# A hybrid RWKV-7, GLA and MLA trunk: all projections of the normalized input in pairs by seven products

## The chip, the cores and the metric

The kernel runs on one core of a Trainium2 chip. The metric is the device time of one execution in microseconds (us). Data and arithmetic are float32.

## The reference, cut to what matters

Two layers run over 640 tokens: 512 of a grid and 128 of a prompt. In each layer the input is normalized and modulated, and one wide matrix w_in projects it to everything that the three branches need. The outputs of the branches are gated by a sigmoid of another part of the same projection, summed, and projected again.

```python
mod = (jax.nn.silu(cvec) @ w_mod + b_mod)[:, None, :]
shift, scale, gate = jnp.split(mod, 3, axis=-1)
h = rmsnorm(x, norm_g) * (1 + scale) + shift
proj = h @ w_in
(rw_r, rw_k, rw_v, rw_wd, rw_ad, rw_g, gl_q, gl_k, gl_v, gl_ad, gl_g,
 ml_qd, ml_kvd, ml_kpe, ml_g, merge) = jnp.split(proj, IN_SPLITS, axis=-1)
...
y_a = (o_a * jax.nn.silu(rw_g)) @ lp['rw_out']      # RWKV-7, forwards and backwards over the tokens
y_b = (o_b * jax.nn.silu(gl_g)) @ lp['gla_out']     # gated linear attention, both ways
y_c = (o_c * jax.nn.silu(ml_g)) @ lp['mla_out']     # attention over a compressed cache
g_a, g_b, g_c = jnp.split(jax.nn.sigmoid(merge), N_BRANCH, axis=-1)
return x + gate * ((g_a * y_a + g_b * y_b + g_c * y_c) @ lp['w_out'])
```

## The kernel before

The normalized input lies in SBUF as hT: 8 tiles of 128 features by 640 tokens. A **unit** is 128 output columns of a projection, 8 weight tiles of 128x128. Units stream from memory through a ring of five slots, unit n in slot n modulo 5; the SP engine asks for unit n when unit n − 5 has been used (L483). On TensorE `project()` makes one unit directly: eight matmuls with 512 columns and eight with 128. ACT copies the 128x640 result out of PSUM; for the gates (items g, gg, mg) ACT makes a sigmoid (L1263) and DVE multiplies it with the value in PSUM (L1552, `gates`).

The order is written out by hand in lists. FIRST_ITEMS are the four units at a layer's start. A layer then goes through four pairs of RWKV heads, **stage p** = 0 to 3. In it BESIDE[p] names four units that TensorE projects while DVE, ACT and a few small matmuls prepare the stage's factors: kkss is the norm sum of the keys, a cumulated decay follows as a scan (L1654), and for each direction d DVE makes the factors, among them the key factor from the activation w_a (L1557 and a product, L1552). When they are done (semaphore dve_fac) TensorE turns them (L585) and works through five token tiles in the steps (0, 1), (2, 3) and (4,). The last step has a long chain of small 64x64 matmuls with DVE and ACT in between; there `project_some` puts pieces of the two units of BESIDE_PROMPT[p] between them, and in layer 0 the modulation weights of the next layer pass through the ring in the same place. At the stage's end DVE finishes the output with a root from ACT and the gate.

Then come the unit kvd, the GLA branch, whose seven levels per quarter have pieces of nine units between them (GLA_FILL), the MLA branch with seven merge units (MLA_MERGE), two at its start and five at fixed steps of its loop, and the output stage. L1439 is ACT's exponential of a level, L1241 and L1245 are the two halves of a root on ACT.

Only the output stage works in pairs: `winograd` takes two units (256 output columns) as a 2x2 block matrix and makes their result by seven products, each of four matmuls with 320 columns, in place of eight block products. For this Pool makes four sums of the weights of a pair, 128x512 each (L523, L525, L526, L530, in `sums`), and once per layer four sums of the blocks of hT (L535 to L540); ACT copies three products and DVE adds the others up in 128x320 corners (`corners`, L1549). Twelve pairs per layer, mb, mc and wo, are made so. Helper lines are one for all: L582 is every matmul, L585 every transpose, L1549 an add, L1552 a product, L1556 and L1557 a scaling, L1560 a scale and add on DVE, L1250 a copy on ACT.

## Time and profile before

| | |
|---|---|
| time, median of 3 runs (lowest, highest) | 2675.94 us (2674.91, 2677.42) |
| the profiled execution, its time | 2676.53 us |
| its span | 2674.7 us |
| mean granted TensorE clock | 0.994 |
| TensorE matmuls busy | 2555.6 us (96%) |
| DVE busy | 1258.9 us (47%) |
| ACT busy | 889.7 us (33%) |
| Pool busy | 182.0 us (7%) |

A share of 96% over the span says which engine is the bound on the whole; it does not say how much idle time stands behind it in a single stage. That is read from the timeline of a stage, where one sees when another engine has its result ready and when TensorE takes it up.

### The profile page before, as it was taken

Reading aid. Unit: us, or ns where it says so; the run is one execution under the profiler, and the core shown is the slowest. Engines: PE = TensorE matmul, PEld = TensorE weight load, DVE = VectorE, ACT = ScalarE, POOL = GpSimd, SP = SyncE. Lnnn points to the kernel's source line nnn. Section 1 sums busy time; section 2 is a strip of 40 time slices with the busy share of each in tenths; the row PEclk is TensorE's granted clock in tenths of the full one; section 3 lists DMA queues with packets and bytes.
Section 4 is the critical chain, followed back from the end, with each engine's and each line's share of the span. In section 5 each row is a group of like instructions: output and inputs, shape, how many; then the busy total and the mean of one; then the engine's idle time right before and its main releaser. Section 6 shows DMA issues by size and latency. Waiting matters only on the chain.

```text
span 2674.7 us, 49682 instructions
## 1 busy us (share of the span) xinstructions
PE 2555.6 (96%) x21544; PEld 1732.9 (65%) x21544; DVE 1258.9 (47%) x2465; ACT 889.7 (33%) x1446; POOL 182.0 (7%) x164
## 2 busy tenths in 40 slices
PE   7999999999999999999999999999999999999997
PEld 3675857667666566666657767685866666566664
DVE  3545536364577444222336464554538735432233
ACT  3424323142454544111024242424334545421111
POOL 0000000000000002221300000000000000122122
PEclk9999999999999999999999999999999999999999
DMA  8102020111110000321321010101011010012212
GB/s 309 41 18 92 7 90 25 62 53 38 69 31 29 26 16 17 118 70 64 111 77 33 10 43 2 50 3 42 10 32 35 29 30 12 25 42 71 63 71 77
DMA packets 34983, 136.61 MB, mean 51 GB/s; under 512 B 4496, under 2 KB 4656, under 8 KB 34128
## 3 DMA queue, kind: packets, MB, share of 16 engines
q1 hardware_dynamic: 31392, 118.18, 13.0%
q0 software_dynamic: 3376, 15.24, 1.6%
q8 instruction: 174, 2.85, 0.4%
q14 instruction: 41, 0.34, 0.0%
HBM read 126.43 MB, written 6.98 MB: 50 GB/s over the span
## 4 chain that ended last, share of the span: by engine, by line
PE 84%; DVE 7%; ACT 5%; issue 2%; DMA 1%; POOL 0%; SPq 0%; ACTq 0%; DVEq 0%; POOLq 0%
PE psum L582 82%; PE psum L585 2%; DMA ring<-units 1%; DVE tmp L1549 1%; DVE m_nm L2046 1%; DVE tmp L1552 1%; ACT tmp L1250 1%; ACT tmp L1502 1%; DVE acts L1549 1%; DVE tmp L1560 1%; DVE tmp L1556 1%; ACT L1245 0%; DVE tmp L1939 0%; ACT L1241 0%; DVE acts L1552 0%
## 5 line engine op out<-in xcount | busy, mean ns | idle before, releaser
L582 PE MATMUL psum<-hT,ring 128*128 128x512 f32 (+2 forms) x3264 | 942.5, 441 | 16.8 <-DMA ring<-units 8.4
L582 PEld LDWEIGHTS psum<-hT,ring 128*128 128x128 f32 x3264 | 523.8, 191 | 418.5 <-issue 375.4
L582 PE MATMUL psum<-tmp 64*64 64x64 f32 (+9 forms) x10624 | 703.9, 259 | 42.6 <-DVE tmp L1552 11.4
L582 PEld LDWEIGHTS psum<-tmp 64*64 64x64 f32 (+3 forms) x10624 | 553.9, 149 | 159.0 <-issue 57.9
L1250 ACT ACTIVATE tmp<-psum 128x512 f32<-128x512 f32 (+7 forms) x490 | 252.7, 519 | 1006.7 <-PE psum L582 932.4
L1250 ACT ACTIVATE acts<-psum 128x640 f32<-128x640 f32 (+4 forms) x206 | 109.4, 531 | 320.0 <-PE psum L582 297.6
L582 PE MATMUL psum<-acts,ring 128*128 128x512 f32 (+1 forms) x768 | 210.8, 434 | 0.0
L1549 DVE TENSOR_TENSOR tmp<-psum,tmp 128x256 f32<-128x256 f32 (+2 forms) x184 | 75.7, 412 | 243.0 <-PE psum L582 208.3
L1549 DVE TENSOR_TENSOR tmp<-tmp,psum 128x320 f32<-128x320 f32 x120 | 56.4, 486 | 264.2 <-PE psum L582 202.1
L582 PEld LDWEIGHTS psum<-acts,ring 128*128 128x128 f32 x768 | 118.6, 191 | 94.7 <-issue 92.1
L1549 DVE TENSOR_TENSOR tmp<-tmp 128x320 f32<-128x320 f32 (+2 forms) x214 | 135.6, 660 | 5.0
L582 PE MATMUL psum<-tmp,ring 128*128 128x320 f32 x448 | 124.8, 432 | 0.0
L585 PE MATMUL psum<-con_sb,tmp 128*128 128x128 f32 x696 | 107.2, 279 | 14.3 <-DVE tmp L1556 13.9
L582 PE MATMUL psum<-acts 64*64 64x64 f32 (+3 forms) x2448 | 109.8, 228 | 5.9 <-DVE acts L1549 3.8
L2046 DVE TENSOR_REDUCE m_nm<-psum 128x1 f32<-128x768 f32 (+1 forms) x80 | 65.8, 822 | 100.7 <-PE psum L582 99.7
L582 PEld LDWEIGHTS psum<-tmp,ring 128*128 128x128 f32 x448 | 85.0, 190 | 35.1
L1716 DVE COPY_PREDICATED tmp<-masks_sb,psum 128x512 f32<-128x512 uint8 x160 | 105.4, 723 | 0.7
L582 PE MATMUL psum<-tmp,acts 128*128 128x320 f32 (+2 forms) x576 | 104.4, 350 | 0.6
L1552 DVE TENSOR_TENSOR tmp<-tmp,acts 128x320 f32<-128x320 f32 (+1 forms) x160 | 88.6, 586 | 34.5 <-ACT tmp L1439 29.1
L582 PEld LDWEIGHTS psum<-acts 64*64 64x64 f32 (+2 forms) x2448 | 93.9, 138 | 12.0 <-DVE acts L1549 9.7
L585 PEld LDWEIGHTS psum<-con_sb,tmp 128*128 128x128 f32 x696 | 78.4, 141 | 35.0 <-DVE tmp L1556 24.2
L1502 ACT ACTIVATE tmp<-psum,m_nm 128x768 f32<-128x768 f32 (+1 forms) x80 | 63.6, 795 | 90.7 <-DVE m_nm L2046 83.7
(164 smaller groups left out, 2157.7 us busy)
## 6 DMA issues: line engine op xcount, KB each, us to landing
ring<-units SPq DMA_DIRECT2D x210, 512.0 KB, 3.6
small_sb<-small SPq DMA_DIRECT2D x1, 2944.0 KB, 13.3
small_sb<-small POOLq DMA_DIRECT2D x1, 2944.0 KB, 11.3
hT<-xT SPq DMA_DIRECT2D x2, 1280.0 KB, 7.3
tmp<-xT POOLq DMA_DIRECT2D x8, 320.0 KB, 5.2
x_keep<-hT POOLq DMA_DIRECT2D x8, 320.0 KB, 4.2
tmp<-x_keep POOLq DMA_DIRECT2D x8, 320.0 KB, 3.4
yT<-acts POOLq DMA_DIRECT2D x8, 320.0 KB, 3.2
```

The source lines that it names most:

```text
L582: return nc.tensor.matmul(out, lhsT, rhs, start=start, stop=stop, skip_group_check=True)
L585: return nc.tensor.transpose(out, in_, ident[p, p])
L1250: nc.scalar.activation(out, src, ACT.Copy).then_inc(act_e.sem, act_e.mark(key))
L1502: nc.scalar.activation(m_p[n % 3][:, 0:w], psum[:, at:at + w], ACT.Exp, bias=m_nm[:, n:n + 1], accum_out=m_sum[:, n:n + 1]).then_inc(act_e ...
L1549: return V.tensor_tensor(out, a, b, op)
L1552: return V.tensor_tensor(out, a, b, ALU.mult)
L1556: return V.tensor_scalar(out, a, s1, None, op0)
L1560: return V.scalar_tensor_tensor(out=out, in0=a, scalar=s, in1=b, op0=op0, op1=op1)
L1716: return V.copy_predicated(gbuf(s % 2, name, 4).rearrange("p (d h) x -> p d h x", d=2), masks[:, m, :, :].unsqueeze(2).broadcast_to([P, 2, ...
L2046: V.reduce_max(m_nm[:, n:n + 1], psum[:, at:at + w], AX.X, negate=True).then_inc(dve_nm.sem, dve_nm.mark(l, h, i))
```

## The change

Of the units that project hT only wdad stays direct. The other 44 of a layer go as 22 pairs by the seven products, and the twelve pairs of the output stage stay pairs. On TensorE `product()` takes the place of `project`, `project_some` and `winograd`; the order of the products is 1, 2, 5, 4, 6, 3, 7, and 5 of the 22 pairs are spread in single matmuls over the GLA levels, 4 over the (4,) steps. FIRST has one pair, BESIDE[p] two, PROMPT[p] one, LAST one, GLA_FILL five, MA three.

Pool makes four weight sums for each pair, so `sums` runs from a layer's start. It also takes from DVE the key factor (`keys`), the product of a gate with its sigmoid (`gated`) and ten memsets per layer. DVE takes from Pool the four sums of hT, now at the layer's start, and adds up the corners of each pair (`corner`): five adds of 128x320. ACT copies three products of 320 columns per pair, and makes the sigmoids of gates in places of their own.

The ring slot of a unit is now worked out ahead (`ring_slots`): the two units of PROMPT[p] in layer 0 keep their slots through the (4,) step while the modulation units pass through the other three. The weights that only MLA reads (wq, wk, wv and the cache ckv, 3328 of 5888 columns of the layer's small weights) are loaded by four transfers on Pool's queue after the GLA branch, into space that is free by then.

```diff
-_small = (("w2a2", 1024), ("gla_a2", 512), ("wq", 2048), ("wk", 512), ("wv", 512), ("ckv", PAST),
-          ("s_rw", 8 * 64), ("s_gla", 4 * P))
+_small = (("w2a2", 1024), ("gla_a2", 512), ("s_rw", 8 * 64), ("s_gla", 4 * P))
...
 
-FIRST_ITEMS = [("wdad", 0), ("k", 0), ("r", 0), ("v", 0)]
-BESIDE = [[("k", 1), ("r", 1), ("v", 1), ("g", 0)], [("v", 2), ("k", 3), ("r", 3), ("g", 1)],
-          [("gq", 0), ("gq", 1), ("gk", 0), ("g", 2)], [("gv", 1), ("gv", 2), ("gv", 3), ("g", 3)]]
-BESIDE_PROMPT = [[("k", 2), ("r", 2)], [("v", 3), ("misc", 0)], [("gk", 1), ("gv", 0)], [("qd", 0), ("qd", 1)]]
-END_ITEMS = [("kvd", 0)]
-GLA_FILL = [("gg", 0), ("gg", 1), ("gg", 2), ("gg", 3), ("mg", 0), ("mg", 1), ("mg", 2), ("mg", 3), ("ma", 4)]
-FILL_START = KT
-FILL_TURN = (2, 2, 6, 2)
-FILL_LEVEL = ((2,) * 7, (2,) * 7, (2,) * 7, (2,) * 5 + (0, 0))
-MLA_MERGE = [("ma", n) for n in (0, 1, 2, 3, 5, 6, 7)]
-MLA_MERGE_AT = (0, 10, 20, 25, 30)
...
+WDAD = ("wdad", 0)
+FIRST = (("k", 0), ("r", 0))
+BESIDE = [[(("v", 0), ("k", 1)), (("r", 1), ("v", 1))], [(("r", 2), ("v", 2)), (("k", 3), ("r", 3))],
+          [(("misc", 0), ("gq", 0)), (("gq", 1), ("g", 2))], [(("gv", 0), ("g", 3)), (("gv", 1), ("gv", 2))]]
+PROMPT = [(("k", 2), ("g", 0)), (("v", 3), ("g", 1)), (("gk", 0), ("gk", 1)), (("gv", 3), ("qd", 0))]
+LAST = (("qd", 1), ("kvd", 0))
+GLA_FILL = [(("gg", 0), ("gg", 1)), (("gg", 2), ("gg", 3)), (("mg", 0), ("mg", 1)), (("mg", 2), ("mg", 3)),
+            (("ma", 4), ("ma", 5))]
+MA = [(("ma", 0), ("ma", 1)), (("ma", 2), ("ma", 3)), (("ma", 6), ("ma", 7))]
+MB, MC, WO = ([((n, 2 * i), (n, 2 * i + 1)) for i in range(PAIRS)] for n in ("mb", "mc", "wo"))
...
+
+
+PRODUCTS = (("1", "11", "11"), ("2", "12", "21"), ("5", "s1", "t1"), ("4", "22", "t4"),
+            ("6", "s2", "t2"), ("3", "s4", "22"), ("7", "s3", "t3"))
+PIECES = 4 * len(PRODUCTS)
+
+PLACES = ["first"] + [(q, j) for q in range(4) for j in range(-1, 7)]
+FILL = {"first": 16}
...
+def ring_slots():
+
+
+    rank = {n: n for n in range(len(STREAM))}
+    for p in range(PAIRS):
+        last = max(INDEX[m, ("mod", 4 * j + 3)] for m, j in MOD_BESIDE[2 * p:2 * p + 2])
+        for it in PROMPT[p]:
+            rank[INDEX[0, it]] = last + 0.5
+    held, slot, turn, before = [None] * RING, [], [], []
+    times = [0] * RING
+    for n in range(len(STREAM)):
+        s = min(range(RING), key=lambda s: -1 if held[s] is None else rank[held[s]])
+        slot.append(s)
+        before.append(held[s])
+        turn.append(times[s])
+        held[s] = n
+        times[s] += 1
+    return slot, turn, before
+
...
+            def sums(l, pr, parts):
+
+                q, n = quarters(l, pr), ORDER.index((l, pr))
+                if 1 in parts:
+                    for it in pr:
+                        u = INDEX[l, it]
+                        pool.wait_ge(s_unit[RING_SLOT[u]], 16 * (RING_TURN[u] + 1))
+                    if n:
+                        pool.wait_ge(filled.sem, filled[wk(*ORDER[n - 1], "5")])
+                    nc.gpsimd.tensor_tensor(q["s1"], q["s3"], q["22"], ALU.add).then_inc(pool_ws.sem, pool_ws.mark(wk(l, pr, "1")))
+                    pool.wait_ge(pool_ws.sem, pool_ws[wk(l, pr, "1")])
+                    if n:
+                        pool.wait_ge(filled.sem, filled[wk(*ORDER[n - 1], "6")])
+                    nc.gpsimd.tensor_tensor(q["s2"], q["s1"], q["11"], ALU.subtract).then_inc(pool_ws.sem, pool_ws.mark(wk(l, pr, "2")))
+                    nc.gpsimd.tensor_tensor(q["s3"], q["11"], q["s3"], ALU.subtract).then_inc(pool_ws.sem, pool_ws.mark(wk(l, pr, "3")))
+                if 4 in parts:
+                    pool.wait_ge(pool_ws.sem, pool_ws[wk(l, pr, "2")])
+                    pool.wait_ge(filled.sem, filled[wk(l, pr, "2")])
+                    nc.gpsimd.tensor_tensor(q["s4"], q["12"], q["s2"], ALU.subtract).then_inc(pool_ws.sem, pool_ws.mark(wk(l, pr, "4")))
+
+            def gated(l, name, i, sig):
+
+                ready(pool, l, (name, i))
...
+                def keys(p, d):
+
+                    pool.wait_ge(act_e.sem, act_e[("za", l, p, d)])
+                    ready(pool, l, ("k", p))
+                    o = fac[:, 4 * d + K_, :]
+                    nc.gpsimd.tensor_scalar(o, w_a, v("k_a", p), omka[:, p:p + 1], ALU.mult, ALU.add).then_inc(pool_k.sem, pool_k.mark(l, p, d, 0))
+                    pool.wait_ge(pool_k.sem, pool_k[l, p, d, 0])
+                    nc.gpsimd.tensor_tensor(o, o, item("k", p), ALU.mult).then_inc(pool_k.sem, pool_k.mark(l, p, d, 1))
+
+                pool.wait_ge(dve_ht.sem, dve_ht[l, "t1"])
                 for p in range(PAIRS):
+                    sums(l, BESIDE[p][0], (1, 4))
+                    sums(l, BESIDE[p][1], (1,))
+                    keys(p, 0)
+                    sums(l, BESIDE[p][1], (4,))
+                    keys(p, 1)
+                    sums(l, PROMPT[p], (1, 4))
                     pool.wait_ge(dve_new_state.sem, dve_new_state[l, p])
                     pool.dma_start(a["new_rw"][l, p], st_t.rearrange("p a b -> p (a b)")).then_inc(s_sto, 16)
+                    gated(l, "g", p, fac[:, 0, :])
...
+                late = a["late"][l]
+                pool.dma_start(m_wv, late[:, LATE["wv"]:LATE["wv"] + 512]).then_inc(s_late[l], 16)
+                pool.dma_start(m_ckv, late[:, LATE["ckv"]:LATE["ckv"] + PAST]).then_inc(s_late[l], 16)
+                pool.dma_start(m_wk, late[:, LATE["wk"]:LATE["wk"] + 512]).then_inc(s_late[l], 16)
+                pool.dma_start(area(0, 2048), late[:, 0:2048]).then_inc(s_late[l], 16)
...
+            def product(l, pr, pieces, parts=h_parts, part_ready=h_ready):
+
+                q = quarters(l, pr)
+                for n in pieces:
+                    m, s, part = PRODUCTS[n // 4]
+                    k = n % 4
+                    if n == 0:
+                        for it in pr:
+                            unit(l, it)
                     if k == 0:
-                        grown["item_at"] = ticket(pe, key, 2, "dve" if it[0] in GATES else "act")
-                        hold(grown["item_at"], 2)
-                        grown["item_w"] = unit()
-                        unit_done()
-                    at = grown["item_at"]
-                    last = wide(at, grown["item_w"][:, k, :], hT[:, k, :], k == 0, k == KT - 1)
-                    if k == KT - 1:
-                        last.then_inc(filled.sem, filled.mark(key))
-                        release(at, 2)
+                        if m in "67":
+                            at = grown[pr, "1"]
+                            pe.wait_ge(dve_mid.sem, dve_mid[wk(l, pr, {"6": "11", "7": "12"}[m])])
+                        else:
+                            at = ticket(pe, wk(l, pr, m), 1, "dve" if m in "13" else "act")
+                            hold(at)
+                        if m in "5637":
+                            pe.wait_ge(pool_ws.sem, pool_ws[wk(l, pr, {"5": "1", "6": "2", "3": "4", "7": "3"}[m])])
+                        grown[pr, m] = at
+                    at = grown[pr, m]
+                    part_ready(l, part, k)
...
+                def corner(pr, to, cs):
+
+                    at1, at3 = place(wk(l, pr, "1")), place(wk(l, pr, "3"))
+
+                    def add(o, at, other=None):
+                        return ttn(o, o if other is None else other, psum[:, at:at + HT], ALU.add)
+
+                    for c in cs:
+                        if c == "11":
+                            dve.wait_ge(act_e.sem, act_e[wk(l, pr, "2")])
+                            add(to[0][:, 0:HT], at1).then_inc(dve_mid.sem, dve_mid.mark(wk(l, pr, "11")))
+                        elif c == "mid":
+                            dve.wait_ge(act_e.sem, act_e[wk(l, pr, "5")])
+                            dve.wait_ge(filled.sem, filled[wk(l, pr, "6")])
+                            add(to[0][:, HT:T], at1, to[1][:, HT:T]).then_inc(dve_mid.sem, dve_mid.mark(wk(l, pr, "12")))
+                        elif c == "12":
+                            dve.wait_ge(dve_mid.sem, dve_mid[wk(l, pr, "12")])
+                            dve.wait_ge(filled.sem, filled[wk(l, pr, "3")])
+                            add(to[0][:, HT:T], at3).then_inc(dve_e.sem, dve_e.mark(wk(l, pr, "3")))
+                        else:
+                            dve.wait_ge(filled.sem, filled[wk(l, pr, "7")])
+                            add(to[1][:, HT:T], at1)
+                            dve.wait_ge(act_e.sem, act_e[wk(l, pr, "4")])
+                            add(to[1][:, 0:HT], at1).then_inc(dve_e.sem, dve_e.mark(wk(l, pr, "1")))
+
+                CORNERS = ("11", "mid", "12", "2")
+
```

On Pool at the start of a layer: this is what stood in its queue from the last setup operation on; each new_rw transfer ends one stage p.

```order
7 L494 CAST masks_sb<-tmp 128x3072 [waits masks_loaded,pool_g1]
8 L495 MEMSET gate 128x5
9 L498 DMA new_rw<-tmp 128x256 [waits dve_new_state] x4
10 L502 DMA new_gla<-tmp 128x512 [waits dve_emptied]
11 L504 MEMSET tmp 32x896 [waits dve_gla_done]
```

Now the same queue holds this between the two pairs of BESIDE[0] and the end of stage 0 (L567 to L576 are the four sums of a pair, L606 and L608 the key factor, L619 the transfer).

```order
20 L571 TENSOR_TENSOR w_sums<-w_sums,ring 128x512 [waits psum_filled,pool_weight_sums]
21 L572 TENSOR_TENSOR ring<-ring 128x512
22 L606 TENSOR_SCALAR tmp<-tmp,vec_sb,omka 128x640 [waits dve_emptied,act_emptied]
23 L608 TENSOR_TENSOR tmp<-tmp,acts 128x640 [waits pool_k]
24 L576 TENSOR_TENSOR ring<-ring,w_sums 128x512 [waits psum_filled,pool_weight_sums]
25 L606 TENSOR_SCALAR tmp<-tmp,vec_sb,omka 128x640 [waits dve_emptied,act_emptied]
26 L608 TENSOR_TENSOR tmp<-tmp,acts 128x640 [waits pool_k]
27 L567 TENSOR_TENSOR w_sums<-ring 128x512 [waits psum_filled,unit1_loaded,unit0_loaded]
28 L571 TENSOR_TENSOR w_sums<-w_sums,ring 128x512 [waits psum_filled,pool_weight_sums]
29 L572 TENSOR_TENSOR ring<-ring 128x512
30 L576 TENSOR_TENSOR ring<-ring,w_sums 128x512 [waits psum_filled,pool_weight_sums]
31 L619 DMA new_rw<-tmp 128x256 [waits dve_new_state]
```

Where Pool had nothing to do but the transfer, it now has twelve weight sums and four key operations per stage, with waits for TensorE (psum_filled) and ACT (act_emptied) among them.

On DVE in stage 0, from the first use of the scan's result to the scan of the second direction, it was:

```order
36 L1549 TENSOR_TENSOR tmp<-tmp 128x640 [waits dve_step]
37 L1552 TENSOR_TENSOR tmp<-tmp 128x640 [waits act_emptied]
38 L1557 TENSOR_SCALAR tmp<-tmp,vec_sb,omka 128x640
39 L1552 TENSOR_TENSOR tmp<-tmp,acts 128x640 [waits dve_step]
40 L1552 TENSOR_TENSOR tmp<-tmp,acts 128x640 [waits act_ex,dve_step]
41 L1560 SCALAR_TENSOR_TENSOR tmp<-tmp 128x640
42 L1552 TENSOR_TENSOR tmp<-tmp 128x640 x2
43 L1654 SCALAR_TENSOR_TENSOR tmp<-gate,tmp 128x640 [waits act_emptied]
```

and now it is:

```order
46 L1668 TENSOR_TENSOR tmp<-tmp 128x640 [waits dve_step]
47 L1668 TENSOR_TENSOR acts<-acts,psum 128x320 [waits psum_filled,dve_middle_sum]
48 L1668 TENSOR_TENSOR acts<-acts,psum 128x320 [waits psum_filled]
49 L1668 TENSOR_TENSOR acts<-acts,psum 128x320 [waits act_emptied]
50 L1671 TENSOR_TENSOR tmp<-tmp 128x640 [waits act_emptied]
51 L1671 TENSOR_TENSOR tmp<-tmp,acts 128x640 [waits act_ex,dve_step]
52 L1679 SCALAR_TENSOR_TENSOR tmp<-tmp 128x640
53 L1671 TENSOR_TENSOR tmp<-tmp 128x640
54 L1671 TENSOR_TENSOR tmp<-tmp 128x640 [waits pool_k]
55 L1811 SCALAR_TENSOR_TENSOR tmp<-gate,tmp 128x640 [waits act_emptied]
```

The scaling with omka and the product behind it, the key factor, have left DVE; three adds of corners have come in, and the last product of the direction waits for Pool's key factor (pool_k).

On DVE at the start of MLA, around the norms of the units qd and kvd, it was:

```order
802 L1552 TENSOR_TENSOR tmp<-acts 128x640 x2
803 L1552 TENSOR_TENSOR tmp<-acts 128x640 [waits act_emptied]
804 L1560 SCALAR_TENSOR_TENSOR acts<-acts,vec_sb,tmp 128x640 [waits act_qrs]
805 L1560 SCALAR_TENSOR_TENSOR acts<-acts,vec_sb,tmp 128x640
806 L1560 SCALAR_TENSOR_TENSOR acts<-acts,vec_sb,tmp 128x640 [waits act_kvrs]
807 L1552 TENSOR_TENSOR tmp<-acts,con_sb 32x512 [waits act_emptied,rotary_constants_loaded]
```

and now it is:

```order
879 L1671 TENSOR_TENSOR tmp<-acts 128x640 x3
880 L1668 TENSOR_TENSOR acts<-acts,psum 128x320 [waits act_emptied]
881 L1679 SCALAR_TENSOR_TENSOR acts<-acts,vec_sb,tmp 128x640 [waits act_qrs]
882 L1679 SCALAR_TENSOR_TENSOR acts<-acts,vec_sb,tmp 128x640
883 L1679 SCALAR_TENSOR_TENSOR acts<-acts,vec_sb,tmp 128x640 [waits act_kvrs]
884 L1668 TENSOR_TENSOR acts<-acts,psum 128x320 [waits psum_filled,act_emptied]
885 L1671 TENSOR_TENSOR tmp<-acts,con_sb 32x512 [waits rotary_constants_loaded]
```

Two adds of corners of the pair MA[0] stand between the norms; the second comes behind the norm of kvd, which waits for ACT's root (act_kvrs), and TensorE's last product of the pair waits for it.

## Rows read from the trace of the kernel before

**Rows 1.** the page: busy time of the engines, and the chain that ended last

```profile
PE 2555.6 (96%) x21544; PEld 1732.9 (65%) x21544; DVE 1258.9 (47%) x2465; ACT 889.7 (33%) x1446; POOL 182.0 (7%) x164
...
PE 84%; DVE 7%; ACT 5%; issue 2%; DMA 1%; POOL 0%; SPq 0%; ACTq 0%; DVEq 0%; POOLq 0%
```

**Rows 2.** busy time by stretch: us, each engine (instructions), clock, DMA share, GB/s

```profile
36.48:79.82 43.34, 43.34 (x162) 24.20 (x162) 10.88 (x23) 8.37 (x12) 2.79 (x2) 1.00 0.49 192
...
1072.14:1087.21 15.07, 15.07 (x58) 10.64 (x57) 2.69 (x5) 2.05 (x4) 5.03 (x4) 1.00 0.11 35
...
861.08:882.54 21.46, 20.79 (x79) 11.54 (x77) 8.01 (x13) 15.85 (x17) 2.90 (x5) 1.00 0.09 29
```

**Rows 3.** waits of TensorE: us in total, times, longest us

```profile
PE psum L582 <- DMA ring<-units: 23.7, 12, 12.3
```

**Rows 4.** timeline, stage p = 1: start, us, engine, line, operation

```profile
233.70 0.83 DVE L1552 TENSOR_TENSOR tmp<-tmp 128x640 f32<-128x640 f32 x1
...
235.42 1.25 PE L582 MATMUL psum<-tmp,con_sb 128*128 128x512 f32 x4
...
242.71 1.49 DVE L1654 TENSOR_TENSOR_SCAN tmp<-gate,tmp 128x640 f32<-128x640 f32 x1 [1.34 <-ACT tmp L1309]
...
259.76 1.70 DVE L1552 TENSOR_TENSOR tmp<-tmp 128x640 f32<-128x640 f32 x4
...
265.42 0.71 PE L585 MATMUL psum<-con_sb,tmp 128*128 128x128 f32 x5
```

**Rows 5.** groups by shape on DVE: count, busy us, mean ns, idle before

```profile
L1557 DVE TENSOR_SCALAR tmp<-tmp,vec_sb,omka 128x640 f32<-128x640 f32 x2 | 1.2, 606 | 0.0
...
L1552 DVE TENSOR_TENSOR tmp<-tmp,acts 128x640 f32<-128x640 f32 x4 | 3.3, 827 | 0.3
...
L1549 DVE TENSOR_TENSOR tmp<-tmp,psum 128x320 f32<-128x320 f32 x120 | 56.4, 486 | 264.2 <-PE psum L582 202.1
```

**Rows 6.** timeline where Pool and DVE overlap, three places of layer 0

```profile
1038.02 3.10 POOL L538 TENSOR_TENSOR tmp<-hT 128x1280 f32<-128x1280 f32 x1
...
1039.34 2.21 DVE L1556 TENSOR_SCALAR tmp<-tmp,m_rec 128x768 f32<-128x768 f32 x1
...
1045.68 0.62 DVE L1556 TENSOR_SCALAR tmp<-tmp,m_rec 128x768 f32<-128x768 f32 x1
...
1116.39 1.51 DVE L1549 TENSOR_TENSOR tmp<-tmp 128x640 f32<-128x640 f32 x1
...
1171.64 0.82 DVE L1552 TENSOR_TENSOR tmp<-tmp,psum 128x640 f32<-128x640 f32 x1 [3.84 <-PE psum L582]
...
1172.38 1.27 POOL L525 TENSOR_TENSOR acts<-acts,ring 128x512 f32<-128x512 f32 x1
...
1172.50 1.83 DVE L1549 TENSOR_TENSOR tmp<-tmp 128x640 f32<-128x640 f32 x1
...
1173.61 1.85 POOL L526 TENSOR_TENSOR ring<-ring 128x512 f32<-128x512 f32 x1
```

**Rows 7.** groups by shape on Pool

```profile
L530 POOL TENSOR_TENSOR ring<-ring,acts 128x512 f32<-128x512 f32 x24 | 30.6, 1274 | 292.7 <-PE psum L582 292.6
```

**Rows 8.** GLA levels: two stretches, and DVE's largest group in them

```profile
712.10:785.00 72.90, 69.38 (x571) 49.19 (x571) 60.56 (x120) 34.20 (x43) 0.00 (x0) 1.00 0.10 30
...
785.00:850.80 65.80, 61.86 (x455) 40.89 (x453) 48.95 (x104) 33.86 (x40) 0.54 (x1) 0.97 0.11 34
...
L1552 DVE TENSOR_TENSOR tmp<-tmp,acts 128x320 f32<-128x320 f32 x56 | 24.8, 484 | 15.0 <-ACT tmp L1439 15.0
```

**Rows 9.** timeline at the start of MLA, ACT and DVE

```profile
873.82 1.28 ACT L1245 ACT_TABLE_LOAD   x1
...
880.03 0.88 DVE L1560 SCALAR_TENSOR_TENSOR acts<-acts,vec_sb,tmp 128x640 f32<-128x640 f32 x1 [2.47 <-ACT tmp L1245]
```

**Rows 10.** timeline of TensorE in a (4,) step of layer 0

```profile
359.54 1.32 PE L582 MATMUL psum<-hT,ring 128*128 128x512 f32 x4 [2.02 <-DMA ring<-units]
```

**Rows 11.** the page: DMA issues, KB each, us to landing

```profile
small_sb<-small POOLq DMA_DIRECT2D x1, 2944.0 KB, 11.3
```

606 lines of the change are left out of this document (323 added, 283 removed).

## The prediction

> **What bounds the kernel now.** I read the page first: the matmuls are busy for 96% of the span and the chain that ended last is 84% TensorE, while DVE is busy 47% and Pool 7% [rows 1]. So TensorE's own work sets the time, and time comes off where its work shrinks, as long as the other engines keep up. The waits of TensorE say how often they don't: 23.7 us on weight loads from memory (12.3 of them in one wait), more than on any other thing [rows 3]. The question is then how near DVE is to being late in each stage, since the change gives DVE and Pool more to do. For that I read stages: the stretch of one head pair [rows 4], the GLA levels [rows 8], the start of MLA [rows 9]. In the first, DVE works almost without a gap from 242.7 on, its last factor is done at 261.5, and TensorE, busy all through, asks for it at 265.4: **4.0 us of cover, no more** [rows 4].
>
> **The price of a pair.** Five direct projections take 43.34 us, 8.67 each; the seven products of a pair of units take 15.07, 2.15 each [rows 2]. A pair saves 17.34 − 15.07 = 2.27 us of TensorE. 22 pairs per layer are converted: 44 × 2.27 = 100 us over both layers if everything else hides. It does not, so I go stage by stage; first as if engines didn't disturb each other, then with what they cost each other.
>
> **Start of a layer (p = 0).** Before the first norm sum (kkss) stand five projections, 43.3 us; now wdad and ten products, 8.7 + 21.5 = 30.2: 13.1 sooner. From there DVE's chain to the last factor grows. Nine adds of corners lie in it, 0.486 each from PSUM = 4.4; the keys leave it, two times 0.61 + 0.83 = 2.9 [rows 5]; but DVE now waits for Pool's two keys, and Pool's own 128x512 operation takes 1.27 [rows 7], so a 128x640 one about 1.6: a pair of them 3.0 against some 1.8 of DVE work beside it, 1.2 late, twice 2.4. Sum +3.9, just inside the 4.0 of cover; with what follows the turns I take −12.4 for the stage. The sums of h on DVE, the memsets on Pool and the smaller first load lie under the projections: nothing.
>
> **Stages p = 1 to 3.** Here TensorE's three products would reach kkss 2.2 sooner, but the square that it needs ended at 234.5, only 0.9 us before TensorE took it up at 235.4 [rows 4], so at most 0.9 can be won; and now a corner (0.49) and a wait for Pool's gate product (about 1.6) stand ahead of that square on DVE. I take kkss 1.8 later, bounds −1 (Pool done early) and +3, and the chain's +3.9 under its cover: +1.8 each.
>
> **(4,) steps.** Two projections become one pair under a chain of small matmuls: −2.27, less some 0.5 that I allow for more switches between large and small matmuls: −1.8 each (bounds −2.3 and −1), four per layer. In layer 0 TensorE waits there for a unit from memory, 2.0 us each time [rows 10]; with both units held ahead this goes: −8 more (bounds −8 and 0).
>
> **GLA start.** One projection gives way to a pair, so 15.07 for 8.67 (+6.4; one unit moved here from the start). Product 5 waits for Pool's first sum, which stands behind the gate product of p = 3, and that behind ACT's last root: 2.2, bounds 0 and 5. Sum +8.6, layer 1 +9.2.
>
> **GLA levels.** 8 direct fills (69.4) become five pairs less four products (66.7); DVE's waits for the activation engine's gates go, corners (20 adds, 9.7 us) replace eight gate products of 0.83 (6.6). DVE is busy 60.6 of 72.9 us and 48.9 of 65.8 [rows 8]. Two products of TensorE's 2.15, and a part of DVE's 15.0 us of waits for ACT [rows 8], which the gates' table loads lengthen: I take −4.5, bounds −8 and +3.
>
> **MLA start.** Two projections (17.3) become one pair, −2.3. But ACT, busy 15.9 of the 21.5 us there [rows 2], gets four sigmoids of some 0.75 and a table load of 1.28 [rows 9] ahead of its copies and of the roots of the norms, 4.3 us, and the fourth waits for Pool, which has just issued four transfers. Copy 2 and with it product 6 come some 3.3 late; the corner that product 7 needs stands on DVE behind the last norm of kvd, which already waits for ACT's root until 880.0 [rows 9], and loses the same again and more: 5.3. Sum +6.3, I take +6.5, bounds 0 and +9. The late weights, 1.7 MB, are asked for at about 851; 2.9 MB took 11.3 us from that queue [rows 11], and TensorE wants them from 883 on: nothing, while the start of MLA is not cut by 20 us.
>
> **MLA loop and outputs.** Five projections become two pairs: 43.35 − 30.14 = −13.1. Outputs −0.5: the last corner is one add shorter [rows 5].
>
> Sum without disturbance: layer 0 −12.4 + 5.4 − 7.2 − 8 + 8.6 − 4.5 + 6.5 − 13.1 − 0.5 = −25; layer 1 −12.4 + 5.4 − 7.2 + 9.2 − 4.5 + 6.5 − 13.1 − 0.5, with 2 us for the longer wait in its p stages, −15. Together **−40**.
>
> **What DVE and Pool cost each other.** This is the step that turns the sign. In the trace they overlap in only a few places, and there both get slow. A DVE scaling of 128x768 takes 0.62 alone and 2.21 while Pool adds [rows 6]: 1039.34 + 2.21 = 1041.55, and Pool's operation had ended at 1041.12. A DVE sum of two SBUF tiles of 128x640 takes 1.83 against 0.82, begun 0.12 after a Pool operation, and the Pool operation behind it takes 1.85 against 1.27; the DVE product that reads PSUM, in the same place, keeps its 0.82 [rows 6]. So two operations on SBUF tiles exclude each other and the later one waits: the price to DVE was 1.01 here, 0.69 at 1116.39 and 1.59 for the scaling. Until now Pool is busy for 7% of the span [rows 1], with sums from the end of the MLA loop on, where DVE has gaps between its waits. After the change it works through the p stages: eight sums of BESIDE, four of PROMPT and four keys each, of which some ten fall between kkss and the last factor, where DVE has no cover left. Ten times 0.85 (the middle, since some meet a PSUM read or a gap) = **8.5 us per p stage**, bounds 4 (every second one falls well) and 12.7 (1.27 each). Eight such stages: 68. GLA start +3 and levels: 24 Pool operations at 0.85 = 20, of which DVE's idle 29 us take half: +10. MLA start +1, loop +2.2. Per layer 50, together **+100** (bounds +45 and +150).
>
> The Trainium skill, page "SBUF — State Buffer", section "Who interferes with whom", says that a DVE instruction with two SBUF inputs and a Pool instruction that reads SBUF share one port pair as a lock, which the first holds for its whole instruction while the other is blocked. The trace agrees (2.21 and 1.85). By that rule each Pool operation costs a gapless DVE chain its full 1.27; that is rival C.
>
> Forecast: −40 + 100 = +60 on the profiled run of 2676.5, which lies 0.6 above the median of 2675.94: **2736**.
>
> **Rivals.**
> A. The collisions are cheap: Pool's sums, which wait for products 5 and 6 of the pair before, fall into DVE's gaps or PSUM reads, at under 0.2 us each. For it: DVE waits for 1.3 us just ahead of the scan at 242.7 and has more gaps before [rows 4]. Against: ten Pool operations take 13 us and don't fit into them. It gives −40, with +20 at most: **2636 to 2656**, faster. The point of decision is a price of 0.34 us per Pool operation (40 of the 100).
> B. Everything hides, the stalls at the starts of GLA and MLA too: −100 to −80, **2576 to 2596**. Against: DVE's wait for ACT until 880.0 [rows 9] and the 4.0 us of cover.
> C. The full price: DVE's chain has no gap where Pool works, and each of the ten operations costs it Pool's own 1.27 [rows 7]: 8 × 10 × 0.42 = +34 on the forecast, **2770**; more if stalls at the starts of GLA and MLA reach their bounds. Against: the adds of corners read PSUM and don't collide.
>
> **How the numbers follow.** Forecast with its own range of 2690 to 2760: 0.5. A 0.27; B 0.06; C and more, from 2760 on: 0.12, half of it above 2772; 0.05 between A and the forecast, within 5 us of 2676. The range reaches from A's lower end to C: 2630 to 2772. A measurement of this kernel can tell 0.2%, 5.4 us, from no change. Slower by more: 0.62; within: 0.05; faster: 0.33.
>
> **What would show it.** Right: TensorE's busy time about 100 us lower (2456) while the span grows; DVE sums of two SBUF tiles in the p stages with a mean well over 0.83 (1.2 or more) and PSUM adds at 0.49; Pool sums at 1.6 instead of 1.3; TensorE waiting for DVE's factors 6 to 10 us in each of eight stages; kkss of layer 0 near 67 us; the loop of MLA 13 shorter. Wrong: if the p stages grow by under 3 us each, collisions don't count and A holds; if TensorE has waits at products 5 and 6 on Pool, then it is Pool's queue, not DVE, that is late; if the GLA levels grow by over 15, DVE was bound there too.

## The result: 2809.92 us, five per cent slower

| | before | changed |
|---|---|---|
| time, median (lowest, highest) of 4 runs each | 2675.43 us (2674.48, 2677.42) | 2809.92 us (2806.96, 2814.54) |
| ratio, 95% interval | | 1.0503 (1.0485 to 1.0521) |
| span of the profiled execution | 2674.7 us | 2805.2 us |
| mean granted TensorE clock | 0.994 | 0.962 |

The forecast was 2736 with a range to 2772. The sign was right; 134.5 us came on top instead of 60. The page of the changed kernel, its busy times, the granted clock in 40 slices and the chain that ended last, answers to [rows 1]:

```profile
PE 2532.5 (90%) x21192; PEld 1789.7 (64%) x21192; DVE 1438.0 (51%) x2617; ACT 879.6 (31%) x1502; POOL 509.1 (18%) x416
...
PEclk9999999999999999999999999899999999999998
...
PE 71%; DVE 16%; ACT 7%; issue 4%; DMA 1%; POOL 1%; SPq 0%; ACTq 0%; DVEq 0%; POOLq 0%
```

TensorE's busy time fell by 23 us and not by the 100 that the fewer matmuls are worth, and its idle time grew from 119 to 273 us. The share of DVE in the chain went from 7 to 16%. What TensorE waited for (total, times, longest) answers to [rows 3]:

```profile
PE psum L702 <- DVE acts L1668: 90.7, 33, 7.6
PE psum L702 <- DVE tmp L1671: 37.1, 27, 5.6
PE psum L702 <- issue: 26.0, 9, 4.8
PE psum L702 <- DVE tmp L1903: 17.1, 12, 3.8
PE psum L702 <- DMA ring<-units: 14.6, 8, 12.3
```

The wait for weights has shrunk as forecast, from 23.7. The largest wait is new: L1668 on `acts` is DVE's add of a corner, and the sum had priced it at the start of MLA only.

To see where the time went, I cut both traces at the same places: where TensorE begins to turn the finished factors of a stage (L585 before, L705 now). For each stretch, the difference of the two spans in us stands beside the forecast's own terms, the 8.5, 3, 10, 1 and 2.2 for Pool and DVE among them; the last column is the mixed version (e12 below) against before. The first row varies with the arrival of the first weights: e11 does the same work there as e12 and had −7.6. The stretch of the GLA levels ends at the turns of the branch's fourth quarter; the rest of the branch is in the row behind it.

| stretch | forecast | changed | e12 |
|---|---|---|---|
| start to turns of p = 0, layer 0 | −3.9 | −5.0 | −1.3 |
| three periods to turns of p = 3, layer 0 | 3 × 6.5 | +11.5, +12.3, +9.8 | −3.9, −2.0, −2.2 |
| the same, layer 1 | 3 × 9.2 | +13.6, +13.4, +14.4 | −2.1, −1.9, −1.8 |
| (4,) of p = 3 and start of GLA, layers 0, 1 | +7.8, +10.4 | +17.8, +15.1 | +4.7, +7.0 |
| GLA levels, layers 0, 1 | +5.5, +5.5 | +18.8, +26.4 | +1.0, +2.7 |
| end of GLA to start of layer 1's p = 0 turns | −7.8 | −7.1 | −21.8 |
| end of GLA of layer 1 to the end | −3.9 | −10.3 | −15.2 |
| sum | +61 | +131 | −37 |

**One stage from close by.** The timeline of p = 1, which answers to [rows 4] (start, us, engine, line, operation, what it waited for):

```profile
226.65 1.55 POOL L582 TENSOR_TENSOR acts<-acts,tmp 128x640 f32<-128x640 f32 x1 [9.53 <-ACT tmp L1363]
226.84 1.70 DVE L1675 TENSOR_SCALAR tmp<-acts,vec_sb 128x640 f32<-128x640 f32 x1
228.16 1.51 POOL L567 TENSOR_TENSOR w_sums<-ring 128x512 f32<-128x512 f32 x1
229.76 4.61 PE L702 MATMUL psum<-hT,w_sums 128*128 128x320 f32 x8 [3.01 <-issue]
234.16 2.10 PE L702 MATMUL psum<-tmp,con_sb 128*128 128x512 f32 x4
...
244.19 2.44 DVE L1811 TENSOR_TENSOR_SCAN tmp<-gate,tmp 128x640 f32<-128x640 f32 x1
245.28 2.04 POOL L606 TENSOR_SCALAR tmp<-tmp,vec_sb,omka 128x640 f32<-128x640 f32 x1
247.58 2.05 DVE L1668 TENSOR_TENSOR tmp<-tmp,sraw 128x640 f32<-128x640 f32 x1
...
262.57 0.48 DVE L1668 TENSOR_TENSOR acts<-acts,psum 128x320 f32<-128x320 f32 x1
263.11 4.13 PE L702 MATMUL psum<-h_sums,w_sums 128*128 128x320 f32 x8 [6.65 <-DVE acts L1668]
267.35 0.49 DVE L1668 TENSOR_TENSOR acts<-acts,psum 128x320 f32<-128x320 f32 x1 [4.29 <-PE psum L702]
270.08 1.55 DVE L1671 TENSOR_TENSOR tmp<-tmp 128x640 f32<-128x640 f32 x2
...
271.89 0.73 PE L705 MATMUL psum<-con_sb,tmp 128*128 128x128 f32 x5 [0.35 <-DVE tmp L1671]
```

Four things stand here. **Collisions:** the scaling of 0.55 took 1.70, the scan of 1.49 took 2.44, the add of 0.82 took 2.05, each beside an operation of Pool. **Pool's queue:** product 5 waited 3.01 for Pool's first sum, which stood behind the gate product (L582), which waited for ACT. **A round trip:** product 6 of the second pair waited 6.65 for the add of corner 11. In the order of DVE this add stands behind the second scan; the next add waits in turn for product 6, and the last factors stand behind it. Each engine waited for the other: TensorE 6.65, DVE 4.29.
```profile
260.00:264.00 4.00, 0.89 (x2) 0.70 (x3) 3.02 (x3) 1.31 (x3) 1.11 (x1) 0.50 0.00 0
264.00:268.00 4.00, 4.00 (x12) 2.62 (x11) 0.66 (x2) 1.10 (x4) 0.00 (x0) 0.67 0.00 0
```

The Trainium skill, page "TensorE: Matmul & The Clock Gate", section "What's actually happening", says that the throttled state is the default and activity releases it; the 0.50 here agrees.

Measured from the turns of p = 0, the norm sum kkss is 3.7 later than before, the first scan 6.5, the second 9.9, the last factor about 15; 3.6 of that went into the cover of 4.0 that I had read, so the cover was real. All four stages of layer 0 have such a wait of 6.6 us at product 6; in layer 1 the same product began at 1483.96, 1643.91, 1803.67 and 1964.40, each after 7.59.

Behind the turns stands a fifth place that the forecast did not have. In layer 0 four scalings of 64x64, which took 1.05 together, took 3.92 beside Pool's sums of the next pair (3.0 to 3.2 in the stages p = 2 and 3, and 1.05 in layer 1), and TensorE waited for what comes after them (L1903, 17.1 us in all):

```profile
105.97 1.27 POOL L567 TENSOR_TENSOR w_sums<-ring 128x512 f32<-128x512 f32 x1 [11.75 <-PE psum L705]
106.20 3.92 DVE L1675 TENSOR_SCALAR tmp<-small_sb,tmp 64x64 f32<-64x64 f32 x4
107.32 1.27 POOL L571 TENSOR_TENSOR w_sums<-w_sums,ring 128x512 f32<-128x512 f32 x1
113.35 2.05 PE L702 MATMUL psum<-con_sb,tmp 64*64 64x64 f32 x32 [3.81 <-DVE tmp L1903]
```

Groups by shape on DVE and Pool (count, busy us, mean ns, idle before), against [rows 5, 7]: adds from PSUM kept their 0.48, operations on SBUF tiles went from 0.83 to a mean of 1.01 and more, Pool's sums from 1.27 up to 1.49.

```profile
L1668 DVE TENSOR_TENSOR tmp<-tmp,psum 128x320 f32<-128x320 f32 x120 | 56.3, 486 | 270.2 <-PE psum L702 210.0 <-ACT tmp L1341 60.1
L1671 DVE TENSOR_TENSOR tmp<-tmp 128x640 f32<-128x640 f32 x80 | 79.3, 1007 | 19.2 <-ACT tmp L1336 18.6
L1671 DVE TENSOR_TENSOR tmp<-tmp,acts 128x640 f32<-128x640 f32 x32 | 41.7, 1322 | 2.8 <-ACT tmp L1423 2.4 <-ACT g_dec L1516 0.2
L572 POOL TENSOR_TENSOR ring<-ring 128x512 f32<-128x512 f32 x68 | 101.1, 1486 | 0.0
```

At the start of MLA, in answer to [rows 9], stand the two waits that the forecast had priced, product 6 behind ACT's copies and product 7 behind the norms:

```profile
941.77 4.01 PE L702 MATMUL psum<-h_sums,w_sums 128*128 128x320 f32 x8 [2.49 <-DVE acts L1668]
946.03 3.47 DVE L1679 SCALAR_TENSOR_TENSOR acts<-acts,vec_sb,tmp 128x640 f32<-128x640 f32 x2 [4.32 <-ACT tmp L1336]
...
951.77 3.77 PE L702 MATMUL psum<-h_sums,ring 128*128 128x320 f32 x8 [3.74 <-DVE acts L1668]
```

### The profile page after: what moved, and what is told of

Its sections match the earlier page's. It is cut to its first block, busy times and chain, and to the rows that moved or that the text cites. A ratio compares the mean times of both kernels' runs of the same rounds, so it can differ in the third digit from the quotient of the medians.

```text
span 2805.2 us, 50011 instructions
## 1 busy us (share of the span) xinstructions
PE 2532.5 (90%) x21192; PEld 1789.7 (64%) x21192; DVE 1438.0 (51%) x2617; ACT 879.6 (31%) x1502; POOL 509.1 (18%) x416
## 3 DMA queue, kind: packets, MB, share of 16 engines
q1 hardware_dynamic: 31392, 116.35, 12.3%
## 4 chain that ended last, share of the span: by engine, by line
PE 71%; DVE 16%; ACT 7%; issue 4%; DMA 1%; POOL 1%; SPq 0%; ACTq 0%; DVEq 0%; POOLq 0%
PE psum L702 69%; DVE tmp L1671 4%; DVE tmp L1668 3%; PE psum L705 2%; DVE acts L1668 2%; DVE tmp L1679 1%; DVE tmp L1811 1%; DVE tmp L2218 1%; DVE tmp L1675 1%; ACT tmp L1628 1%; ACT tmp L1341 1%; DMA ring<-units 1%; ACT L1336 1%; ACT L1332 1%; ACT tmp L1408 0%
## 5 line engine op out<-in xcount | busy, mean ns | idle before, releaser
L702 PE MATMUL psum<-hT,ring 128*128 128x320 f32 (+2 forms) x1504 | 452.8, 447 | 6.2 <-DVE hT L1676 6.1
L702 PEld LDWEIGHTS psum<-hT,ring 128*128 128x128 f32 x1504 | 281.1, 195 | 133.9 <-issue 31.6
L576 POOL TENSOR_TENSOR ring<-ring,w_sums 128x512 f32<-128x512 f32 x68 | 88.4, 1300 | 1283.1 <-PE psum L702 1283.0
L702 PE MATMUL psum<-h_sums,ring 128*128 128x320 f32 x960 | 290.2, 443 | 8.3 <-DVE acts L1668 7.6
L702 PE MATMUL psum<-h_sums,w_sums 128*128 128x320 f32 x480 | 170.7, 504 | 72.8 <-DVE acts L1668 72.8
L702 PEld LDWEIGHTS psum<-h_sums,ring 128*128 128x128 f32 x960 | 181.3, 193 | 86.2 <-DVE acts L1668 8.7
L1341 ACT ACTIVATE acts<-psum 128x320 f32<-128x320 f32 (+4 forms) x278 | 122.6, 448 | 263.4 <-PE psum L702 240.4
L1668 DVE TENSOR_TENSOR acts<-acts,psum 128x320 f32<-128x320 f32 (+1 forms) x300 | 121.0, 429 | 159.3 <-PE psum L702 82.4
L1668 DVE TENSOR_TENSOR tmp<-tmp,psum 128x320 f32<-128x320 f32 x120 | 56.3, 486 | 270.2 <-PE psum L702 210.0
L1668 DVE TENSOR_TENSOR tmp<-psum,tmp 128x256 f32<-128x256 f32 (+2 forms) x184 | 75.6, 411 | 224.9 <-PE psum L702 223.6
L702 PE MATMUL psum<-hT,w_sums 128*128 128x320 f32 x480 | 158.6, 472 | 25.2 <-issue 25.2
L702 PEld LDWEIGHTS psum<-h_sums,w_sums 128*128 128x128 f32 x480 | 102.1, 220 | 121.4 <-DVE acts L1668 78.3
L1668 DVE TENSOR_TENSOR tmp<-tmp 128x320 f32<-128x320 f32 (+2 forms) x214 | 147.8, 717 | 5.0
L702 PEld LDWEIGHTS psum<-hT,w_sums 128*128 128x128 f32 x480 | 95.7, 205 | 68.2 <-issue 36.9
L705 PE MATMUL psum<-con_sb,tmp 128*128 128x128 f32 x696 | 108.8, 282 | 26.1 <-ACT tmp L1628 8.7
L567 POOL TENSOR_TENSOR w_sums<-ring 128x512 f32<-128x512 f32 x68 | 94.0, 1382 | 194.8 <-DMA ring<-units 91.0
```

What stands on the lines that cost most here:

```text
L567: nc.gpsimd.tensor_tensor(q["s1"], q["s3"], q["22"], ALU.add).then_inc(pool_ws.sem, pool_ws.mark(wk(l, pr, "1")))
L576: nc.gpsimd.tensor_tensor(q["s4"], q["12"], q["s2"], ALU.subtract).then_inc(pool_ws.sem, pool_ws.mark(wk(l, pr, "4")))
L702: return nc.tensor.matmul(out, lhsT, rhs, start=start, stop=stop, skip_group_check=True)
L705: return nc.tensor.transpose(out, in_, ident[p, p])
L1341: nc.scalar.activation(out, src, ACT.Copy).then_inc(act_e.sem, act_e.mark(key))
L1668: return V.tensor_tensor(out, a, b, op)
```

## Experiments

Each kernel is the changed one with the edit shown. Every group of experiments had runs of the kernel before beside it, with medians of 2674.3 to 2676.9 us; differences are of medians. Where an interval is given it is that of the ratio to before. e1 to e4 and e6 to e8 have two runs each, so a difference of under some 8 us to or between them is not clear of noise; the others have four to eight.

**Do Pool's weight sums cost the time?** e1 shrinks them to four columns.

```diff
+                if pr[0][0] not in ("mb", "mc", "wo"):
+                    q = {name: z[:, 0:1, 0:4] for name, z in q.items()}
```

> The changed kernel, with Pool's weight sums of the 22 hT pairs of each layer shrunk to 1x4 elements per partition: they stay in the queue with all their waits, but do almost no work (the products made from them are left out in that sense: their weights are not the sums). Keys, gate products and the sums of the output stage stay whole. Theory P (Pool and DVE excluding each other costs most of what was lost): the 176 sums cost DVE about 0.85 us each in chains, so the time falls by 90 us or more, to 2720 or less. Theory R (a round trip: product 6 of the second pair of each p stage waits for the corner 11 that stands on DVE behind the second scan, and DVE then waits for product 6): the sums cost only what DVE's rows show in stage 0, some 4 us per p stage and as much in the GLA levels, so 40 to 60 us less, 2750 to 2770, and TensorE's wait of 6.6 us at product 6 stays above 3.

2720.75 us (1.0165, 1.0136 to 1.0195): 89 less. The products made from these sums are no longer the right ones; in a row they still take TensorE 2.32 us each. The wait at product 6 fell from 6.65 to 4.2 us in stage p = 1, so it is there without Pool's sums too. DVE is busy 1344.2 us instead of 1438.0, so 94 us of DVE's time were nothing but waiting inside its instructions. But is it the shared access, or Pool being late? e13 leaves Pool busy for nearly as long as it was, with memsets in place of sums:

```diff
+                for part, z in (("a", out), ("b", out)):
+                    pool.memset(z, 0.0).then_inc(pool_ws.sem, pool_ws.mark(wk(l, pr, part + m)))
...
+                return pool.memset(out[:, :, 0:64], 0.0)
```

> Changed kernel; each weight sum of the 22 pairs of hT is replaced by three memsets of Pool on the same place, 1152 columns in all, some 1.3 us by the mean of Pool's 512-column memsets (0.526), with the same waits ahead and the same marks behind. The sums are zeros, so the values are not the reference's. Pool is as long busy as before and its results come at the same time, but it reads nothing. Theory P (two engines that read SBUF tiles exclude each other): like the shrunken sums, 2720 to 2735, DVE busy near 1345. Rival L (Pool's results come late, its own time counts): 2795 to 2815, DVE busy lower all the same or not. Between, 2750 to 2790: a memset of Pool disturbs DVE too, or both causes share the 89 us.

2734.49 (1.0219, 1.0205 to 1.0233): 75 less, with Pool busy for 490.4 us against 509.1. Its page:

```profile
PE 2518.5 (92%) x21192; PEld 1780.3 (65%) x21192; DVE 1350.5 (49%) x2617; ACT 878.8 (32%) x1502; POOL 490.4 (18%) x768
```

and the group of DVE that had 1007 ns is back at its old mean:

```profile
L1680 DVE TENSOR_TENSOR tmp<-tmp 128x640 f32<-128x640 f32 x80 | 65.5, 835 | 19.1 <-ACT tmp L1345 18.6
```

In the timeline of e13, 31 DVE sums and products on two SBUF tiles of 128x640 run beside a memset of Pool, and each takes 0.82 or 0.83. Not every group is back: the 84 adds of 128x640 have a mean of 1024 ns, 953 in the changed kernel; Pool's key factors and gate products still read SBUF there. So of the 89 us, about 75 go with what Pool's reads do to DVE, and about 14 with Pool's own time in the chain. The Trainium skill, page "SBUF — State Buffer", section "Who interferes with whom", states that a DVE instruction with two SBUF inputs contends with a GpSimd instruction that reads SBUF and not with one that only writes it; 1438 against 1350 us agrees.

e9 adds instead of taking away: two more sums behind the fourth of 13 pairs per layer, whose result nobody reads.

```diff
+                    if pr in [FIRST] + [x for b in BESIDE for x in b] + PROMPT:
+                        for extra in "98":
+                            nc.gpsimd.tensor_tensor(acts[:, 22, 0:512].rearrange("p (a b) -> p a b", a=4), w_sums[:, 0], w_sums[:, 1], ALU.add).then_inc(pool_ws.sem, pool_ws.mark(wk(l, pr, extra)))
...
```

> One thing added to the changed kernel: behind the fourth weight sum of each of the 13 pairs of a layer in FIRST, BESIDE and PROMPT, Pool makes two more sums of the same size (128x512) into a free place that nobody reads. 52 operations, some 68 us of Pool time, and no engine waits for them. Theory P (a Pool sum costs DVE, and through it the time, where both run on SBUF tiles): the shrunken sums of the first experiment took 89 us off for 176 sums, 0.5 each, so 52 x 0.5 = +26 us on 2810, about 2836, with the periods p = 1 to 3 some 3 to 4 us longer each. Rival L (the cost is only that sums come late for TensorE's products): the extra sums stand behind the fourth one and Pool is idle 80% of the time, so under +5 us, 2810 to 2815. Full lock price (1.27 each): +66, 2876.

2821.05 (1.0525 to 1.0561): 11 more, not the 26 of theory P, and more than rival L allows. Per sum that is 0.21 of time and 0.38 of DVE's busy time (1457.6), against 0.51 and 0.53 in e1. A price per sum does not carry over from one place to another: how much of it reaches the end depends on what DVE has to do just there.

**The round trip.** e2 puts the add of corner 11 (and ACT's copies that it needs) ahead of the second scan.

```diff
+                        if d == 1:
+                            corner(BESIDE[p][1], items(BESIDE[p][1]), ("11",))
                         dve.wait_ge(act_e.sem, act_e[("zw", l, p, d)])
```

> The changed kernel with one thing moved: the corner 11 of the second BESIDE pair is added ahead of the scan of direction 1 and not behind it (ACT's copy of product 2 moves ahead with it). Theory R: product 6 no longer waits (now 6.6 to 7.6 us in eight stages), DVE no longer waits 4.1 us for product 6, and TensorE's clock doesn't fall there; 4 to 6 us per stage, 32 to 48 in all, so 2762 to 2778. Theory P: DVE's chain is as long as before but for the order, so at most 10 us less, about 2800.

2771.19 (1.0324 to 1.0384): 39 less. The same place in its timeline:

```profile
253.28 2.42 PE L702 MATMUL psum<-h_sums,w_sums 128*128 128x320 f32 x8 [0.45 <-DVE acts L1669]
...
267.74 1.30 PE L705 MATMUL psum<-con_sb,tmp 128*128 128x128 f32 x5 [5.84 <-DVE tmp L1672]
```

Product 6 goes on after 0.45, in 2.42. TensorE's waits did not shrink, they moved: 1.63 at product 7 and 5.84 at the turns. There DVE's last three operations took 1.88 and 3.68 (two of them) instead of 0.82 each, beside three sums of Pool from 261.5 on. What is won, 4.9 us per stage, is DVE's own wait of 4.29 and the slow product behind TensorE's.

**The clock.** e3 makes product 4 of the second pair twice more, which fills the wait ahead of product 6 with matmuls nobody needs.

```diff
+                    if k == 0 and m == "4" and (l, pr) in [(l, BESIDE[p][1]) for p in range(PAIRS)]:
+                        for again in range(4 * 2):
+                            mm(psum[:, at:at + HT], q[s][:, again % 4, :], parts[part][:, again % 4, :], again % 4 == 0, again % 4 == 3)
```

> The changed kernel with product 4 of the second BESIDE pair of each p stage made three times over (the same result; 8 more matmuls, 4.3 us, in the 6.6 us in which TensorE waits for the corner 11). Theory C (part of the loss is TensorE's clock, which falls after such a wait: product 6 then takes 4.0 to 4.6 us in place of 2.2): product 6 takes 2.2 to 3 us, TensorE's granted clock rises over the 0.962 of the changed kernel, and the time falls by 1.5 to 2.4 us per stage, 12 to 20 in all, to about 2793. If the clock is no part of it, or the work is added to the path: the same or up to 10 us more.

2797.11 (1.042 to 1.0481): 128 matmuls more by the trace's count and 13 us less, at a mean granted clock of 0.970.

```profile
253.02 6.62 PE L702 MATMUL psum<-h_sums,ring 128*128 128x320 f32 x24
261.99 2.42 PE L702 MATMUL psum<-h_sums,w_sums 128*128 128x320 f32 x8 [2.34 <-DVE acts L1671]
```

Product 6 began after 2.34 of wait and took 2.42 instead of 4.13, in all stages of layer 0; in layer 1 a wait of 3.3 is left, and behind it the product took 2.42 to 4.63. That a wait can cost more than its length is shown by this; how much of the missing 77 us of TensorE's busy time it explains in all is not, since e3 touches one wait of several.

**Keys on Pool.** e4 gives the key factor back to DVE; e6 is e4 with the early corner.

```diff
-                    keys(p, 0)
...
+                        ts(fac[:, 4 * d + K_, :], w_a, v("k_a", p), omka[:, p:p + 1], ALU.mult, ALU.add).then_inc(dve_step.sem, dve_step.mark())
...
+                        mul(fac[:, 4 * d + K_, :], fac[:, 4 * d + K_, :], k_).then_inc(dve_step.sem, dve_step.mark())
```

> The changed kernel with the key factor back on DVE (a scaling and a product of 128x640 per direction, 1.43 us, as before the change); Pool makes none. Theory P: the four key operations on Pool cost DVE more than they save (3.0 us of Pool work against 1.43), so the p stages get 1 to 2.5 us shorter each, 8 to 20 in all. If moving them was right: DVE's chain grows by 2.9 per stage, up to 23 us more, 2833.

> The changed kernel, whole, with the corner 11 ahead of the second scan and the key factor back on DVE: 39 + 7 = 46 us less than the changed kernel, about 2764, if the two add up; 2770 if the keys only mattered while DVE waited.

e4: 2802.51 (1.0441 to 1.0501), 7 less, which is just under theory P's 8 to 20 and not clear of noise; e6: 2756.25 (1.0263 to 1.0345), 54 less, where e2 and e4 together have 46. So the keys on Pool cost some 7 us (e4) to 15 (e6 against e2); both point the same way, and neither shows that moving them saved time. DVE's busy time did not even grow (1431.8 against 1438.0) when it took over 32 operations, so it must have lost as much in waits inside its other instructions before. e5 puts e1, e2 and e4 together.

> The changed kernel with three things at once: the weight sums of the hT pairs shrunk to 1x4 (left out of the computation, as in the run with small sums), the corner 11 ahead of the second scan, and the key factor back on DVE. If these causes are separate, their gains add up: 89 + 39 + 7 = 135 us less than the changed kernel, 2675, as long as the kernel before. If two of them are the same waits seen twice (DVE late at the corner 11 because Pool held it up), the gain is smaller, 100 to 115, about 2700. TensorE's granted clock should come back to 0.98 or more.

2681.1 (1.001 to 1.0032), 129 less, where the three alone have 135: they add up to within the noise, and bring the kernel back to where it was before the change. They do not bring the gain: the forecast had −40 for a kernel in which DVE and Pool don't disturb each other, and this one stands 6 above before. What is left is in the GLA branch. Its levels took 140.0 us there, 128.0 before (141.6 and 126.3 in layer 1), at a granted clock of 0.94:

```profile
687.00:827.00 140.00, 126.30 (x897) 91.61 (x896) 101.17 (x198) 55.66 (x78) 12.60 (x21) 0.94 0.11 37
```

The (4,) step of p = 3 with the start of GLA took 10.2 and 13.4 more than before, while the periods of p are 0.6 to 3.7 shorter than before in layer 0 and within 1.0 of it in layer 1.

**Which pairs are worth it?** A pair made directly costs TensorE 2.27 more and frees DVE and Pool. e7 makes all of BESIDE directly (with e4), e8 also LAST and GLA_FILL; e10 only LAST and GLA_FILL (with e2). In these three the direct units read hT where t1 stands, so their values differ from the reference's.

```diff
+DIRECT = [x for b in BESIDE for x in b]                       # e7
+DIRECT = [x for b in BESIDE for x in b] + GLA_FILL + [LAST]   # e8
+DIRECT = GLA_FILL + [LAST]                                    # e10
```

> The changed kernel with the eight BESIDE pairs of each layer made as direct projections again (16 units; no weight sums, no corners for them; they read hT in which one block holds a difference, so their values are not the reference's) and the key factor on DVE. This undoes the change in the p stages alone. Forecast: the period from one p stage to the next comes down from 160 to 167 us to the 146 to 154 of the kernel before less 2 to 4 for the pair of the (4,) step: 151 in layer 0, 145 in layer 1; eight stages and the way into GLA give 90 to 110 us, so 2700 to 2720. If Pool's work for PROMPT alone kept DVE late, less than half of that.

> As the run with direct BESIDE units, and the pairs LAST and GLA_FILL direct as well; pairs stay for FIRST, PROMPT, MA and the output stage (values as in that run). It undoes the change in the GLA levels too, which grew by 18.8 and 26.4 us, and the way into them. Forecast: 45 to 65 us less than the run with direct BESIDE units, and below the kernel before by what FIRST, PROMPT and MA save without a busy DVE beside them: 2.3 x 2 + 1.8 x 8 + 8 + 13 x 2 = 53, so about 2625 to 2650. If it is not below 2676, the pairs don't pay in those places either.

> Changed kernel with the early corner of the second experiment; the five pairs of the GLA levels and the pair of its start (LAST) are projected directly, the pairs of BESIDE and PROMPT stay pairs. The direct units read hT where t1 has been written, so their values are not the reference's. Theory D (in the GLA levels DVE has no room: corners and Pool's sums cost more than the saved matmuls): levels back near the 125 to 130 us of before from 149, start of GLA 4 to 6 shorter, so 2771 less about 50 = 2715 to 2725. Rival T (the GLA levels wait on the gates' table loads of ACT or on the chain of small matmuls, which stay): the work of TensorE grows by 2 x 13.6 us and less than half of the wait goes, 2760 to 2790.

e7: 2705.49 (1.0075 to 1.0154), 104 less than the changed kernel; e8: 2644.4 (0.9847 to 0.9924); e10: 2712.04 (1.0117 to 1.0147), 59 less than e2. The GLA levels of layer 0 by stretch, before, changed and e10 (columns as above):

```profile
698.00:826.00 128.00, 120.24 (x896) 81.86 (x895) 97.94 (x187) 68.95 (x84) 0.00 (x0) 0.99 0.11 34
```
```profile
745.00:892.00 147.00, 127.57 (x899) 92.47 (x898) 111.64 (x201) 55.66 (x78) 30.82 (x21) 0.93 0.10 34
```
```profile
721.00:850.00 129.00, 126.50 (x929) 85.56 (x928) 97.91 (x180) 59.26 (x78) 13.86 (x7) 1.00 0.12 38
```

With direct fills TensorE is at full clock and has hardly a gap. With pairs it has less to do by its matmuls and still shows more busy time, at a clock of 0.93. One place of the changed kernel shows how: the two sums behind the scan take 4.05 beside Pool's gate products (0.82 each alone), TensorE waits 5.57, and the group behind the wait takes 2.40 instead of 1.33:

```profile
782.63 3.67 POOL L582 TENSOR_TENSOR acts<-acts 128x640 f32<-128x640 f32 x2 [20.91 <-ACT acts L1363]
782.93 4.05 DVE L1668 TENSOR_TENSOR tmp<-tmp 128x640 f32<-128x640 f32 x2
790.00 2.40 PE L702 MATMUL psum<-tmp 64*128 64x64 f32 x20 [5.57 <-DVE tmp L1671]
```

**A version that beats both.** e11 is e8 with the reference's values: t1 lies in a place of its own (two unused items) until the GLA branch ends, and is then written over hT for MA. e12 makes MA[0] directly as well; ACT copies its second unit behind the roots of the norms. e14 is e12 with the first pair of each BESIDE kept as a pair.

```diff
+DIRECT = [x for b in BESIDE for x in b] + GLA_FILL + [LAST]            # e11
+DIRECT = [x for b in BESIDE for x in b] + GLA_FILL + [LAST] + MA[:1]   # e12
+DIRECT = [b[1] for b in BESIDE] + GLA_FILL + [LAST] + MA[:1]           # e14
...
+        t1_first = acts[:, 22:24, :].rearrange("p a (b c) -> p (a b) c", b=2)
```

> A version that is meant to beat both and computes the reference: the pairs of BESIDE, LAST and GLA_FILL are projected directly, those of FIRST, PROMPT and MA stay pairs; t1 lies beside hT until the GLA branch ends and is then written in place; keys are made on DVE. The run before it with the same split, but one place for t1, took 2644. Theory: the extra sum of 128x1280 (about 1.4 us per layer) lies under other work, 2642 to 2650, 0.99 of the kernel before. Rival: it stands ahead of the first MLA pair and costs 3 to 5 us a layer, 2652 to 2655.

> As e11_mixed, but the first MLA pair is direct too, t1 goes in place behind it, and ACT copies its second unit behind the roots of the two norms. Theory (product 6 and 7 of that pair stand behind the norm chain of DVE and ACT, 2.5 us of wait and the slow products behind it): the pair's 2.3 us of extra work are less than the wait and the roots come earlier, 2 to 4 us less per layer than e11, 2635 to 2642. Rival: the wait is hidden elsewhere and the extra work shows, 2.3 more per layer, 2648 to 2655.

> As e12_mixed_ma0 (all of BESIDE direct), but the first pair of BESIDE[p] stays a pair in each of the eight p stages, only the second is direct; it computes the reference. Theory S (the second pair carries the cost: its corner 11 behind a scan that product 6 waits for, and sums of Pool beside the factors): the first pair keeps its 2.27, 8 x 2.27 = 18 less, minus some 0.5 for each of 32 more Pool sums = 16: 2632 to 2640, p stages at 150 to 152. Rival F (the first pair's corners and sums stand ahead of the scans on DVE and delay the factors as much): stages at 154 or more, 2660 or over.

e11: 2643.91 (0.9866 to 0.9896). e12: **2639.76** (ratio 0.9864, 0.9848 to 0.9881), 37 us or 1.4% faster than the kernel before in the runs beside it (2676.88) and 170 faster than the changed one. e14: 2662.01 (0.993 to 0.9961), 22 slower than e12, though TensorE has 8 × 2.27 = 18 us less to do. Theory S missed: its rival F had 2660 or over. Both pairs of BESIDE together cost 97 (e4 against e7) and the first alone 22, so the second carries more, as theory S had it, but the first is no gain either. Its timeline shows the wait of product 5 that stood in the changed kernel too:

```profile
372.54 1.70 DVE L1742 TENSOR_SCALAR tmp<-acts,vec_sb 128x640 f32<-128x640 f32 x1
373.86 1.51 POOL L577 TENSOR_TENSOR w_sums<-ring 128x512 f32<-128x512 f32 x1
375.46 3.93 PE L710 MATMUL psum<-acts,w_sums 128*128 128x320 f32 x8 [3.00 <-issue]
```

The page of e12, whose matmuls fill 96% of the span at a mean granted clock of 0.993:

```profile
PE 2525.1 (96%) x21432; PEld 1733.1 (66%) x21432; DVE 1306.5 (50%) x2501; ACT 885.7 (34%) x1472; POOL 290.1 (11%) x264
```

## Why the prediction was right in sign and short by half

**What held.** The price of a pair: e12 keeps 7 pairs a layer of the 22, 2 × 7 × 2.27 = 32 us, and its TensorE is busy 2555.6 − 2525.1 = 30.5 less. kkss of layer 0 came at 68.12 (forecast near 67). The start of layer 0, −5.0 for −3.9; but by its first weights alone this row differs by 6.3 between e11 and e12, so the match is worth little. MLA: from DVE's last operation of the GLA branch to the first logits the changed kernel took 42.3 us in both layers, before 36.6, so +5.7 (forecast +7.5); the rest of layer 0 with the start of layer 1 −12.9 (−15.3; the 13.1 in it should be 43.35 − 30.14 = 13.2). The (4,) steps, seen in e12: −3.9, −2.0 and −2.2 in layer 0, for which I had 3.8 each, and −1.8 to −2.1 in layer 1 (1.8). Rivals A and B are out: the collisions cost 75 us, and not under 20. Rival C was nearest in number, 2770, but its reason, a higher price per collision, is not what made the rest of the loss.

**Pool and DVE: the right size, in part by luck.** +100 was forecast; 75 to 89 were measured for the weight sums (e13, e1), and 7 to 15 for the keys. The mechanism held. My price of 0.85 for ten of Pool's operations per stage was a fair sum made of wrong parts: a sum cost 0.51 on average over all of them and 0.21 in the places of e9, and it cost also beside scans, beside tiny scalings (3.92 for 1.05) and in the GLA levels. And the sign that I had named, TensorE waiting 6 to 10 us for DVE's factors in each of eight stages, did not come: at the turns it waited 2.1 at most. The waits stood at product 6.

**The undisturbed sum: the step that failed.** With the sums of Pool shrunk the kernel should have stood near −40, a little above it for the keys and gate products that stay on Pool, and it stood at +45 (e1). Three terms were wrong.

*The p stages.* "The chain's +3.9 under its cover: +1.8 each" counted the adds of corners as work of DVE, 0.486 each, and not as a link between two engines. The add of corner 11 waits for nothing, but product 6 waits for it, and the next add and the last factors wait for product 6. I had looked for this loop at the start of MLA, where I priced it with 5.3, and not in the eight p stages, where it stands with waits of 6.6 us and costs 39 us in all (e2). I also bounded kkss at +3 at most; it was 3.7 late, because product 5 waited for Pool's first sum. That wait I had named for the start of GLA and, as a sign, at the end of the prediction, but had given it no price here.

*The clock.* A wait was priced at its length. The timeline shows 19 waits of 2.5 to 7.6 us right ahead of a product that took 3.6 to 4.6 instead of 2.3, and two, of 2.18 and 3.01, ahead of one that took 2.39. My own sign said it: TensorE busy 2456, measured 2532.5. The mean granted clock was 0.962.

*The GLA branch.* Without Pool's part I had −4.5 for the levels, and for the start with the (4,) step ahead of it +4.8 and +7.4. In e5, where Pool's weight sums are gone, the levels still cost +12.0 and +15.3 and the start +10.2 and +13.4. These two make up the 46 us by which e5 stays above my −40: 36 the levels and 11 the start. I had subtracted matmuls and part of a wait from a stage whose DVE was busy 60.6 of 72.9 us [rows 8], and added its 9.7 us of corner adds to no chain. The prediction's last sentence named this case ("if the GLA levels grow by over 15, DVE was bound there too"): they grew by 18.8 and 26.4, and e10 took it back to 129.0. How this divides between corners, the gates' order on ACT and the clock was not separated, and stays open.

## What to carry to other kernels

Count a conversion stage by stage, and by what it asks of the engines beside the one that it relieves: the same 2.27 us per pair were a gain in seven pairs of a layer and a loss in the other fifteen (measured in groups, not pair by pair). For every result that one engine adds to and another reads on, write down who waits next, in both directions; where an instruction in the middle of one engine's dense chain feeds the other engine, which feeds that chain again, the pair of waits is the cost, not the instruction. In these runs work that was moved to Pool was out of DVE's way only where it did not read SBUF while DVE worked on SBUF tiles.

## What the runs showed of the hardware

- Pool memsets of nearly the same total length leave DVE alone (busy 1350.5), Pool sums of SBUF tiles do not (1438.0). Besides sums and products, scans are lengthened (8 of 24 from 1.49 to 2.44), scalings that read one SBUF tile (0.55 to 1.70), and copies of five columns, from 0.17 to 0.68 in all 16 cases of the changed kernel. In e13 the eight scans beside a memset kept their 1.49. The predicated copy with its mask in SBUF and its data in PSUM is not lengthened: 96 of them have a mean of 631 ns before and 630 in the changed kernel.
- Short operations suffer most for their length: four scalings of 64x64, 0.26 each, took 1 us each while Pool worked through three sums.
- TensorE after a wait: after 6.65 us of it, the eight matmuls of a product took 4.13; after 3.01, 4.61 in one place and 2.39 in another; after 2.49, 4.01; after 2.34 and after 0.45, 2.42. So the length of the last wait alone does not decide. The kernel before had a small case: behind a wait of 1.83 at 2132.8 a group of eight with 512 columns took 4.63 instead of 2.43. Filling a wait with matmuls that nobody needs made the kernel faster (e3).
